# The last expert-weight unit of each layer, used by column halves instead of by row halves

## What is computed

```python
def hierarchical_moe(x, w_group, b_group, w_expert, b_expert, w_gate, w_up, w_down):
    ...                                     # top-1 of 4 groups, then top-2 of its 8 experts -> gates (tokens x 32)
    hg = jnp.einsum('btd,edf->btef', x, w_gate)
    hu = jnp.einsum('btd,edf->btef', x, w_up)
    h = jax.nn.silu(hg) * hu * gates[..., None].astype(x.dtype)
    return jnp.einsum('btef,efd->btd', h, w_down)
```

## Time and profile before

| | |
|---|---|
| median of three executions | 1466.05 us (1463.7 to 1466.63) |
| the profiled execution, its own time | 1464.75 us |
| its span | 1463.0 us |
| PE busy (matmul) | 1318.1 us, 90% |
| VectorE, ScalarE, GpSimd busy | 383.6, 317.2, 65.7 us |
| read from HBM | 479.6 MB |
| mean granted clock of TensorE | 0.987 |

### The profile page before, as it was taken

How to read it: one execution, slowest core, us unless ns; L and a number is a source line. 1 busy time by engine, 2 the same in 40 slices (tenths; PEclk the granted TensorE clock), 3 DMA queues, 4 the chain that set the end, 5 groups by cost and what they waited for, 6 DMA issues and landing times.

```text
span 1463.0 us, 18556 instructions
## 1 busy us (share of the span) xinstructions
PE 1318.1 (90%) x7758; PEld 752.2 (51%) x7758; DVE 383.6 (26%) x930; ACT 317.2 (22%) x773; POOL 65.7 (4%) x106
## 2 busy tenths in 40 slices
PE   8999988878999999888789999888789999988875
PEld 7866534332564765333328865343328775533431
DVE  1453311112624844111111133111012461401103
ACT  0233322111322322222112003221111251312210
POOL 2200000000000520000000000000001000000000
PEclk9999999999999999999999999999999999999997
DMA  9656699999835019999998837999998355799995
GB/s 319 265 228 238 226 429 428 426 428 414 370 115 207 25 67 421 429 427 428 428 426 344 381 129 274 429 427 428 427 418 358 118 230 230 294 429 427 428 427 237
DMA packets 36774, 481.99 MB, mean 329 GB/s; under 512 B 4416, under 2 KB 4736, under 8 KB 6864
## 3 DMA queue, kind: packets, MB, share of 16 engines
q1 hardware_dynamic: 35424, 478.19, 79.4%
q0 software_dynamic: 1120, 2.09, 0.7%
q10 hardware_dynamic: 144, 0.46, 0.1%
HBM read 479.60 MB, written 1.05 MB: 329 GB/s over the span
## 4 chain that ended last, share of the span: by engine, by line
PE 76%; DMA 13%; DVE 5%; ACT 4%; issue 2%; SPq 0%; POOL 0%; another core or an unknown queue 0%; DVEq 0%; POOLq 0%
PE psum L781 15%; PE psum L1083 12%; DMA memory<-in_units 10%; PE psum L812 8%; PE psum L837 8%; PE psum L1043 7%; PE psum L1126 7%; PE psum L1118 7%; DMA ring<-in_units 4%; ACT memory L1222 2%; PE psum L820 2%; DVE memory L1900 1%; PE psum L746 1%; PE psum L1179 1%; ACT memory L1414 1%
## 5 line engine op out<-in xcount | busy, mean ns | idle before, releaser
L781 PE MATMUL psum<-memory,ring 128*128 128x256 f32 x1024 | 224.1, 381 | 1.5 <-DMA ring<-in_units 1.1
L781 PEld LDWEIGHTS psum<-memory,ring 128*128 128x128 f32 x1024 | 195.4, 191 | 29.4 <-DMA ring<-in_units 1.5
L1126 PE MATMUL psum<-memory 128*128 128x512 f32 x256 | 125.9, 617 | 42.8 <-DVE memory L1900 22.8
L1043 PE MATMUL psum<-memory,x 128*128 128x128 f32 x1024 | 132.7, 284 | 35.0 <-ACT memory L1222 35.0
L1043 PEld LDWEIGHTS psum<-memory,x 128*128 128x128 f32 x1024 | 121.4, 195 | 73.8 <-issue 70.9
L1083 PE MATMUL psum<-ring,memory 128*32 128x512 f32 x1152 | 134.4, 605 | 15.3 <-DMA ring<-in_units 15.1
L1222 ACT ACTIVATE memory<-psum,affine_t 128x128 f32<-128x128 f32 x312 | 117.3, 457 | 139.0 <-PE psum L1043 131.6
L1895 DVE TENSOR_TENSOR memory<-memory,psum 128x256 f32<-128x256 f32 x32 | 13.5, 420 | 461.3 <-ACT memory L1408 461.3
L837 PE MATMUL psum<-ring,memory 128*128 128x512 f32 x256 | 112.1, 593 | 0.9 <-DVE memory L1495 0.9
L1126 PEld LDWEIGHTS psum<-memory 128*128 128x128 f32 x256 | 43.7, 189 | 129.6 <-DVE memory L1900 48.2
L1083 PE MATMUL psum<-memory 128*32 128x512 f32 x896 | 103.5, 601 | 6.4 <-DMA memory<-in_units 6.4
(11 more groups left out here) (225 smaller groups left out, 1186.7 us busy)
## 6 DMA issues: line engine op xcount, KB each, us to landing
ring<-in_units SPq DMA_DIRECT2D x129, 2048.0 KB, 26.9
memory<-in_units SPq DMA_DIRECT2D x88, 2048.0 KB, 25.7
memory<-in_units SPq DMA_DIRECT2D x16, 1024.0 KB, 28.1
ring<-in_units SPq DMA_DIRECT2D x4, 512.0 KB, 8.6
memory<-in_const SPq DMA_DIRECT2D x3, 448.0 KB, 30.7
x<-in_x SPq DMA_DIRECT2D x2, 512.0 KB, 4.2
out<-x SPq DMA_DIRECT2D x2, 512.0 KB, 2.7
memory<-in_tables SPq DMA_DIRECT2D x1, 640.0 KB, 33.0
```

What stands on the lines that cost most here:

```text
L781: last = nc.tensor.matmul(bank(key, T, s * T), w[:, 2 * m + s, k, :], xT[:, k, :], start=(k == 0), stop=(k == KD - 1))
L1043: last = nc.tensor.matmul(psum[:, to, (at + i) * P:(at + i + 1) * P], x[:, c, k * P:(k + 1) * P], sel[:, par, c, :], start=(c == 0), stop= ...
L1126: last = nc.tensor.matmul(psum[:, 4 + NH * c + h, :], hT[:, FC + c, :], y_sb[:, h * HB:(h + 1) * HB], start=False, stop=last_quad, skip_gr ...
```

## The change

Each layer's last unit (the right output half of the last quad's down weights) is packed a second time, at the end of the array of weights, in the order (column half, j, expert, column), so that each 1 MB transfer brings all rows of 256 output columns. PE uses the halves in two passes, `down_columns(0)` and `down_columns(1)`, each 8 matmuls of 256 columns, into banks 3 and 1. `combine(0)` moves between the two passes. ScalarE copies each half with an instruction of its own, and the right half of z is made by `combine_columns(0)` and `combine_columns(1)`, two matmuls of 256 columns each. `z_ready` is told by the two matmuls of `combine_columns(1)`. The other quads and the path for more tokens stay as they are.

```diff
@@ load(at, *unit), SP
                 elif unit[0] == "moe" and unit[2] == NQ * QU - 1:
+                    at = PACKED + unit[1]
                     for j in range(FC):
@@ quad, PE: down(h)
-                        if j and h == NH - 1 and last_quad and sems is first:
-
-                            pe.wait_ge(half_in, 16 * (n // NQ + 1))
@@ quad, PE: combine(h)
-                        if last_quad and sems is first and h == NH - 1:
-                            last.then_inc(z_ready, 1)
@@ quad, PE
-                if last_quad:
+                half = HB // 2
+
+                def down_columns(b):
+
+                    w = slots[GU + 1][0].rearrange("p (b j e c) -> p b e j c", b=2, e=QE, j=FC)
+                    for j in range(FC):
+                        for e in range(QE):
+                            rows = slice(W * e, W * (e + 1))
+                            last = nc.tensor.matmul(psum[rows, (3, 1)[b], 0:half], hT[:, j, rows], w[:, b, e, j],
+                                                    start=(j == 0), stop=(j == FC - 1))
+                    return last
+
+                def combine_columns(b):
+                    cols = slice(b * half, (b + 1) * half)
+                    return [nc.tensor.matmul(psum[:, 4 + NH * c + 1, cols], hT[:, FC + c, :], y_sb[:, HB:D][:, cols],
+                                             start=False, stop=True, skip_group_check=True) for c in range(TC)]
+
+                if last_quad and sems is first:
+                    l = n // NQ
+                    down(0)
+                    pe.wait_ge(*slots[GU + 1][1])
+                    down_columns(0).then_inc(columns_used, 1)
+                    combine(0)
+                    pe.wait_ge(half_in, 16 * (l + 1))
+                    down_columns(1).then_inc(sems["unit_used"], 1)
+                    pe.wait_ge(columns_ready, l + 1)
+                    combine_columns(0)
+                    pe.wait_ge(sems["y1_ready"], n + (1 + FREE))
+                    for last in combine_columns(1):
+                        last.then_inc(z_ready, 1)
+                elif last_quad:
                     down(0)
                     down(1)
                     combine(0)
@@ quad, ScalarE (by_columns only for the last quad)
-                act.wait_ge(sems["unit_used"], n * QU + (QU + spare(sems)))
-                nc.scalar.activation(y_sb[:, HB:D], psum[:, 3, :], ACT.Copy).then_inc(sems["y1_ready"], 1)
+                if by_columns:
+                    act.wait_ge(columns_used, l + 1)
+                    nc.scalar.activation(y_sb[:, HB:HB + HB // 2], psum[:, 3, 0:HB // 2], ACT.Copy).then_inc(columns_ready, 1)
+                    act.wait_ge(sems["unit_used"], n * QU + QU)
+                    nc.scalar.activation(y_sb[:, HB + HB // 2:D], psum[:, 1, 0:HB // 2], ACT.Copy).then_inc(sems["y1_ready"], 1)
+                else:
+                    act.wait_ge(sems["unit_used"], n * QU + (QU + spare(sems)))
+                    nc.scalar.activation(y_sb[:, HB:D], psum[:, 3, :], ACT.Copy).then_inc(sems["y1_ready"], 1)
@@ packed(inputs)
-    units = np.empty((PACKED, P, UNIT), np.float32)
+    units = np.empty((PACKED + DEPTH, P, UNIT), np.float32)
+        units[PACKED + l] = moe[-1, -1].reshape(P, FC, QE, 2, HB // 2).transpose(0, 3, 1, 2, 4).reshape(P, UNIT)
```

More of the change, by code:

```diff
@@ L431, in build @@
         unit_used, half_ready = sem("unit_used"), sem("half_ready")
+        columns_used, columns_ready = sem("columns_used"), sem("columns_ready")
         pair_gathered, pair_ready = sem("pair_gathered"), sem("pair_ready")
@@ L1403, in first_tokens, with quad @@
                 token_blocks(l, 0, (2, 3), 2).then_inc(first["xw_ready"], 1)
-            def quad(l, sems, n, par, ahead):
+            def quad(l, sems, n, par, ahead, by_columns=False):
                 act.wait_ge(sems["unit_used"], n * QU + (GU + spare(sems)))
@@ L1422, in experts @@
                 for par in range(2):
-                    quad(l, first, l * NQ + NQ - 2 + par, par, par == 0)
+                    quad(l, first, l * NQ + NQ - 2 + par, par, par == 0, par == 1)
             def experts_more(l, runs):
```

## The result

The changed kernel takes 1483.28 us (median of four, 1480.58 to 1484.24) beside 1466.34 for the kernel before: ratio 1.0114, 95% interval 1.0102 to 1.0126, so 17 us slower. The forecast was 1464.0 with a range up to 1466.5.

A forecast was written before the change was run, and what follows sets the result against it. Each layer was taken as a PE-bound mixer, then expert weights streaming at full rate, with serial work after the last half's landing; 0.3 + 1.25 + 0.2 - 0.4 = 1.35 us gained, from 1465.3 to 1464.0, range 1461.0 to 1466.5.

The forecast's parts named there:

- T2 to the right half's statistics: From the last weight half's landing (T2) to L1510 at a layer's end: 3.1 us at full clock, about 4.0 at low.
- The narrow pass at 0.99 to the next start: Each `down_columns` pass on PE: 0.85 us for 16 records plus 0.14, so 0.99.
- the second copy: ScalarE's copy of the second column half: 0.38 us, hidden under `combine_columns(0)` (0.86 us).
- the table load: ScalarE's L1456, 1.28 us, due before L1511 is done: would cost nothing, at worst 0.1.
- Rival B: Narrow passes bound by weight loads: 16 in a row, 1.76 us a pass, net 5.0 lost, 1470.3; chance 0.05.
- Rival D: Halves land together, so 5.5 us instead of 4.3 follows their landing: 1.2 lost in each layer, 1470.1; chance 0.03.
- The single terms of layers 0 to 2: Earlier start of L1510 at the ends of layers 0, 1 and 2: 0.3, 1.25 and 0.2 us gained.
- Layer 3 was to lose 0.4: At layer 3's end PE at the low clock is last, not the DMA: L1510 at 1451.58 against 1451.16.
- rival A: More layers end at the full clock, each gaining 0.9 to 1.7 more; all layers, 1460.3; chance 0.34.
- the sentence of the first part: A microsecond saved between the last half's landing and the stream's restart moves the restart and next landing by the same amount.
- unchanged time from L1510 to the next T2: Expected sign in the changed profile: statistics of the right half to the next layer's last landing take as long as before.
- What rides along: Side effects on ScalarE's copies and table load and on SP's and GpSimd's transfers: nothing, at worst 0.1 for the table load.

The follow-up runs named there:

- e6: Changed kernel with PE's code moved 168 instructions by 15 tiny matmuls at the start and narrower `keep_busy` matmuls in layer 0: 1462.61 us, ratio 0.9974.
- e7: Kernel before with 40 more PE instructions in each layer, by writing four `keep_busy` matmuls as narrower ones with the same columns: 1479.03 us, ratio 1.0084.
- e4: Kernel before without the path for more than 32 tokens of an expert on any engine (no flag load, no jump): 1470.13 us, ratio 1.0033.
- e10: Kernel before with `combine(0)` moved between the two parts of `down(1)`, row halves and number of PE instructions kept: 1463.45 us, ratio 0.9981.
- e8: Kernel before with 48 more PE instructions in layer 0 alone, by writing `keep_busy` matmuls as narrower ones: 1469.87 us, ratio 1.0033.
- e9: Kernel before with 25 tiny matmuls at the start and narrow `keep_busy` in all layers, putting its branches where e6 has them: 1467.40 us, ratio 1.0010.
- e1: Changed kernel with 80 increments of an unused semaphore ahead of PE's first wait: 1474.24 us, ratio 1.0059.
- e2: Kernel before with 40 increments of an unused semaphore on PE in each layer's last quad: 1490.24 us, ratio 1.0171.

## Why the prediction was wrong

**What held.** T2 to the right half's statistics was to be 3.1 us at the full clock and about 4.0 at the low one. It is 3.11 and 3.15 (layers 1 and 3) and 4.10 (layers 0 and 2). The narrow pass at 0.99 to the next start is 1.00 (764.79 to 765.79), the second copy 0.38 under `combine_columns(0)`, the table load hidden. Rival B is refuted: 16 loads take 0.59 us beside a pass of 1.07. The Trainium skill, "TensorE: Matmul & The Clock Gate", section on packing small matmuls, lets weight loads overlap running matmuls only if the row groups differ; the trace disagrees here too, since these tiles share all rows. Rival D too: the halves land 2.4 us apart in layer 1 (764.75 by PE's loads, 767.19). The single terms of layers 0 to 2, 0.3, 1.25 and 0.2, measured 0.2, 1.2 and 0.2. Layer 3 was to lose 0.4 and gained 1.2, as it ended at the full clock in this execution (1.00 from 1466 to 1468), which was rival A's case. In e6, with 2.9 to 3.1 us from T2 to the statistics in all four layers, the whole is 4.8 us against its partner, near what rival A gave for all layers (5.0).

**What failed** is the sentence of the first part, that a microsecond saved there moves the restart of the stream by the same amount, together with the forecast "unchanged time from L1510 to the next T2". The time from the statistics to the transposes was taken over from the kernel before, as if nothing in it depended on the change. The part "What rides along" went through SP's, GpSimd's and ScalarE's queues, and left out PE's own instruction stream: 40 more instructions in a layer were priced by their run time alone. They moved a jump by 40, 80 and 120 places. In the kernel before the target had 51 to 87 instructions left in its block, which covers `keep_busy` and, in part, the transposes; then it had 11, 3 and none. The missed term is 4.3, 7.0 and 8.5 us, 19.8 in sum against 2.9 gained. It wasn't on the list of rivals. It could have been: the diff adds instructions right in front of a branch, and the profile before shows instruction packets on q8 in an otherwise full DMA.

Why the fetch takes so long can be told in part. From T2 to its packet on q8 it is 6.3, 6.0 and 5.9 us in the kernel before, and the jump begins 2.7, 2.5 and 2.5 us behind T2. The rest, from the jump to the packet, depends on the layer:

```
               jump to packet, layers 0 1 2    layer 3    q1 in the first 3 us, layers 0 to 2 / layer 3
before         3.63  3.52  3.46                1.10       415 to 429 GB/s / 0
after          4.49  3.66  4.12                1.01       415 to 429 GB/s / 0
e7             4.40  3.76  4.00                1.01       416 to 429 GB/s / 0
```

In layer 3 nothing is left to load, and in every run with the jump the packet starts 0.98 to 1.16 us after it. So the full data queue is the likely reason for the other 2.4 to 3.7 us; no run changed the queue alone.

What remains open: the 1.2 to 2.1 us between the end of the packet and PE's next matmul, and the medians of e4 and e10. The offset of the count was fitted and not read off; that it then placed the stall of e8 and the absence of any in e6 and e9 is what speaks for it.

## What to carry to other kernels

Before adding or removing instructions ahead of a jump on an engine with little slack behind it, look where the jump and its target stand: a change of code that is right on its own terms can cost several times its gain through the fetch of a block, and can equally be blamed for it wrongly. When a profile shows an engine idle with "issue" and nothing else at a branch, move the code with instructions that cost nothing and measure again before judging the change. And the partner run (the old kernel with the same code places) is what separates the two effects. The order alone (e10), without more instructions, runs no such risk; its median is as good as e6's, but no profile here shows where that comes from.

## What the runs showed of the hardware

Semaphore increments on PE followed each other 0.15 us apart (80 from 1.45 to 13.53 us in e1, 40 from 344.36 to 350.38 in e2), beside matmuls that were still running, and what PE had no work for stood in the chain (8.48 and 3.46 us), so they are no free padding. PE's instructions came in packets of 16 KB on q8, and a jump whose target had less than about a dozen instructions left in its block, or whose own block had been entered 32 or fewer instructions earlier, cost 2.1 to 6.5 us of standing; with 35 and more left, and 68 and more entered, at most 0.4 (the jump 0.98 us long at 68, 0.3 to 0.4 at 112 and more). The block's packet started 3.4 to 4.7 us after the jump while q1 moved 413 to 430 GB/s (e1 aside), and 1.0 to 1.2 us after it in layer 3, while q1 moved nothing. Four narrow matmuls of 128 x 32 against 256 columns run side by side as well as against 512: 16 records in 1.07 us.
